# A two-block transformer kernel on one core: bias rows laid out in another stage, row stores waited for in another stage, and four weight loads issued ahead of sixteen small ones

## What is computed

```
# block 1
mod = silu(c) @ w_ada + b_ada                      # six rows of 1024: shifts, scales, gates
u   = layer_norm(x) * (1 + sc_m) + sh_m
q, k, v, f_logit, xb, gb = split(u @ w_in)
attn = forgetting_attention(q, k, v, f_logit + b_f)
lru  = rg_lru_branch(xb, gb, conv_w, conv_b, w_rg, b_rg, w_ig, b_ig, lru_lambda)
x   = layer_norm(ALPHA * x + (1 + gt_m) * (concat(rms(attn), rms(lru)) @ w_out))
x   = block with a mixture of 16 experts (2 per token), with sh_f, sc_f, gt_f
# block 2
mod_2 = silu(c_2) @ w_mod_2 + b_mod_2              # the same for the second block
bias  = rpb_2[:, row_off, col_off]                 # a relative position bias, looked up per head
...  neighbourhood attention with that bias, grouped attention, 32 experts (4 per token)
```

## Time and profile before

| what | value |
|---|---|
| median of 3 runs | 3181.14 us (3176.08 to 3182.53) |
| profiled execution, its own time | 3176.49 us |
| its span, first to last instruction | 3174.7 us |
| PE busy | 2540.7 us, 80% |
| DVE busy | 2245.4 us, 71% |
| ACT busy | 1558.6 us, 49% |
| POOL busy | 328.6 us, 10% |
| mean granted TensorE clock | 0.897 of full speed |

### The profile page before, as it was taken

The page is one execution under the profiler, slowest core; times in us unless marked ns, Lnnn a source line. Parts: engine busy times, 40 slices in busy tenths (PEclk is TensorE's granted clock), DMA queues, the critical chain, the costliest instruction groups (busy, mean ns, idle before and its releaser), DMA issues. The chain is left out here.

```text
span 3174.7 us, 37782 instructions
## 1 busy us (share of the span) xinstructions
PE 2540.7 (80%) x12807; PEld 2076.3 (65%) x12807; DVE 2245.4 (71%) x2177; ACT 1558.6 (49%) x1451; POOL 328.6 (10%) x277
## 2 busy tenths in 40 slices
PE   2968564499992699577885399999999999999991
PEld 2851554477771499466764377777777777777771
DVE  5546654588786312387844589999999999999985
ACT  2213430277671323255621066677776777777660
POOL 1120200033320000000000001110111111111110
PEclk9979786699996799788987599999999999999995
DMA  5736011499992322100021299999999999999984
GB/s 199 267 122 223 11 60 55 171 359 377 357 374 106 106 80 90 41 1 27 32 102 53 66 323 370 370 366 365 360 366 363 371 370 366 364 366 361 363 342 152
DMA packets 254857, 731.70 MB, mean 230 GB/s; under 512 B 29772, under 2 KB 69931, under 8 KB 252527
## 3 DMA queue, kind: packets, MB, share of 16 engines
q1 hardware_dynamic: 228180, 645.62, 56.3%
q0 software_dynamic: 21984, 80.77, 6.7%
q10 hardware_dynamic: 4608, 4.20, 0.4%
HBM read 692.73 MB, written 39.39 MB: 231 GB/s over the span
## 5 line engine op out<-in xcount | busy, mean ns | idle before, releaser
L48 PE MATMUL psum_all<-sb_ring_r,sb_arena_r 128*128 128x512 f32 (+1 forms) x2912 | 1068.7, 367 | 0.0
L152 DVE TENSOR_TENSOR sb_ring_r<-sb_ring,sb_hi_ring 128x2048 fp32r<-128x2048 f32 x297 | 674.5, 2287 | 251.5 <-ACT sb_hi_ring L143 246.1
L47 PE MATMUL psum_all<-sb_hi_ring,sb_arena_r 128*128 128x512 f32 (+1 forms) x1880 | 663.8, 353 | 49.9 <-DVE sb_ring_r L152 46.6
L49 PE MATMUL psum_all<-sb_hi_ring,sb_arena_r 128*128 128x512 f32 (+1 forms) x1880 | 659.6, 351 | 0.0
L143 ACT ACTIVATE sb_hi_ring<-sb_ring 128x2048 fp32r<-128x2048 f32 x297 | 563.6, 1912 | 107.7 <-DMA sb_ring<-in_w_gu_dram 35.0
L48 PEld LDWEIGHTS psum_all<-sb_ring_r,sb_arena_r 128*128 128x128 f32 x2912 | 556.6, 191 | 91.2
L152 DVE TENSOR_TENSOR sb_ring_r<-sb_ring,sb_arena_r 128x2048 fp32r<-128x2048 f32 x258 | 581.9, 2283 | 29.6 <-ACT sb_arena_r L143 29.1
L143 ACT ACTIVATE sb_arena_r<-sb_ring 128x2048 fp32r<-128x2048 f32 x258 | 484.9, 1910 | 199.7 <-DMA sb_ring<-in_w_gu_dram 194.8
L47 PEld LDWEIGHTS psum_all<-sb_hi_ring,sb_arena_r 128*128 128x128 f32 x1880 | 360.1, 192 | 106.5 <-DVE sb_ring_r L152 47.3
L47 PE MATMUL psum_all<-sb_arena_r 128*128 128x512 f32 x1032 | 417.7, 405 | 12.2 <-DVE sb_ring_r L152 7.0
L49 PE MATMUL psum_all<-sb_arena_r 128*128 128x512 f32 x1032 | 408.4, 396 | 0.0
(11 more groups left out here) (369 smaller groups left out, 3200.7 us busy)
## 6 DMA issues: line engine op xcount, KB each, us to landing
sb_ring<-in_w_gu_dram SPq DMA_DIRECT2D x272, 1024.0 KB, 6.8
sb_ring<-in_w_dn_dram SPq DMA_DIRECT2D x136, 1024.0 KB, 8.9
sb_ring<-in_w_e_gate_dram SPq DMA_DIRECT2D x36, 1024.0 KB, 7.5
sb_ring<-in_w_e_up_dram SPq DMA_DIRECT2D x36, 1024.0 KB, 7.3
sb_ring<-in_w_e_down_dram SPq DMA_DIRECT2D x36, 1024.0 KB, 7.8
sb_ring<-in_w_in_dram SPq DMA_DIRECT2D x27, 1024.0 KB, 5.8
sb_arena<-in_w_ada_dram POOLq DMA_DIRECT2D x16, 1024.0 KB
sb_ring<-in_w_mod_dram SPq DMA_DIRECT2D x16, 1024.0 KB, 5.1
```

Of the source, the lines that this page charges most:

```text
L47: eng.matmul(out, a[0], b[0], start=start, stop=False)
L48: eng.matmul(out, a[0], b[1], start=False, stop=False)
L49: return eng.matmul(out, a[1], b[0], start=False, stop=stop)
L152: dve.tensor_tensor(s.lo[c % SLOTS], s.raw[c % SLOTS], s.hi[c % len(s.hi)].bitcast(F32), ALU.subtract).then_inc(s.lo_made, 1)
```

## The change

Three edits. The first hunk is of `Modulation`, the second of `gates_and_lru` on SP, the third of `sync` in `forgetting_attention`, on SP too.

```diff
 class Modulation:
-    def store(self, pool):
+    def store(self, k, pool):
         for i, job in enumerate(self.jobs):
             if job[7] is not None:
                 pool.wait_ge(self.s.put, i + 1)
+                k.mod_stores += 1
                 pool.dma_start(job[7].rearrange("o (k p) -> p (o k)", p=P), job[5],
-                               allow_slow_non_contiguous=True).then_inc(self.s.stored, 16)
-        if self.rows:
-            pool.wait_ge(self.s.stored, 16 * self.rows)
+                               allow_slow_non_contiguous=True).then_inc(k.mod_stored, 16)
...
+            for n in range(MOD_SLOTS):
+                load_mod(n)
             for w, t in (("w_rg", w_r), ("w_ig", w_i)):
                 for half in range(2):
                     at_rows = slice(half * HW, (half + 1) * HW)
                     for j in range(NJ):
                         sp.dma_start(t[at_rows, j, at_rows], a[w][0, 2 * j + half]).then_inc(s.loaded, 16)
-            for n in range(len(mod_chunks)):
+            for n in range(MOD_SLOTS, len(mod_chunks)):
                 load_mod(n)
-            rows = k.rpb_rows.rearrange("(r i) (h g c) -> h r i g c", i=16, h=NH, c=48)
-            for h in range(NH):
-                for turned_row in range(GRID_H):
-                    first = RPB_PAD + (h * RPB_R + turned_row) * RPB_C - 16
-                    src = bass.AP(k.rpb_pad.tensor, first, [[1, 16], [RPB_C, GRID_H], [1, 48]])
-                    sp.dma_start(rows[h, turned_row], src).then_inc(k.rpb_rows_made, 16)
...
             for i, row in enumerate((2, 6)):
                 sp.dma_start(k.gate_rows[row:row + 1, :], mod_rows[32:33, i * D:(i + 1) * D]).then_inc(s.rows_stored, 16)
+            rows = k.rpb_rows.rearrange("(r i) (h g c) -> h r i g c", i=16, h=NH, c=48)
+            for h in range(NH):
+                for turned_row in range(GRID_H):
+                    first = RPB_PAD + (h * RPB_R + turned_row) * RPB_C - 16
+                    src = bass.AP(k.rpb_pad.tensor, first, [[1, 16], [RPB_C, GRID_H], [1, 48]])
+                    sp.dma_start(rows[h, turned_row], src).then_inc(k.rpb_rows_made, 16)
             sp.wait_ge(s.rows_stored, 48)
+            sp.wait_ge(k.mod_stored, 16 * k.mod_stores)
```

More of the change, by code:

```diff
@@ L294, in __init__ @@
         self.jobs, self.acc, self.psum, self.slots = jobs, acc, psum, slots
-        self.s = sems(nc, ctx, name, "used", "acc", "summed", "put", "stored", "chain")
+        self.s = sems(nc, ctx, name, "used", "acc", "summed", "put", "chain")
         self.landed = [nc.alloc_semaphore(name=f"{name}_landed{i}") for i in range(len(slots))]
@@ L304, in __init__ @@
         self.per = -(-len(self.steps) // turns)
-        self.rows = sum(job[7] is not None for job in jobs)
     def ready(self, u):
@@ L406, in _ @@
         def _(pool):
-            m.store(pool)
+            m.store(k, pool)
 def normalise(nc, k, name, src, ntt, width, dst, centre, eps, gain=None, bias=None, store=None, gate=None):
@@ L575, in _ @@
                 mod.load(pool)
-                mod.store(pool)
+                mod.store(k, pool)
         @block.sync
@@ L2652, in program @@
         k.rpb_rows = nc.dram_tensor("rpb_rows", (P, NH * GRID_H * 48), F32).ap()
+        k.mod_stored, k.mod_stores = nc.alloc_semaphore(name="mod_stored"), 0
         k.rpb_rows_made = nc.alloc_semaphore(name="rpb_rows_made")
```

## The result

| | before | after |
|---|---|---|
| median | 3178.61 us (4 runs, 3173.87 to 3182.53) | 3145.51 us (4 runs, 3140.77 to 3148.98) |
| ratio | | 0.9895, 95% interval 0.988 to 0.991 |
| span of the profiled execution | 3174.7 us | 3147.2 us |
| mean granted clock | 0.897 | 0.899 |

The change saves 33 us of the median; the spans of the two profiled executions differ by 27.5.

What follows compares the result with a forecast made beforehand. PE is busy 80%, mostly in untouched experts; the edits act on barrier-closed stages between 200 and 412 us, by who ends last. 24.4 + 7.8 + 2.6 = 34.8 us saved, giving 3141.7 to 3146.3, forecast 3145, range 3131 to 3151.

Steps and rivals of the forecast that it cites:

- Edit A: SP's 64 bias row DMAs move from the gate stage's end to the attention: ACT then ends the stage, 24.4 us saved.
- The cover in the attention: Attention work on PE, ACT and DVE hides SP's 64 issues: 55.6 us available, 41.1 needed.
- rival 4: SP issues the 64 DMAs more slowly and ends the attention; gain shrinks from 0.87 us each, slower from 1.41; chance 0.02.
- Edit C: In the gate stage, four chunk loads go ahead of the gate weights: 7.8 us saved on PE's chain.
- The pause: PE's wait for the first weight chunk in the gate stage, after the forget gate: 4.67 us to be saved.
- four take 13.2: PE's first four chunks in the gate stage take 13.2 us at full clock instead of 16.35, saving 3.1 us.
- Edit B: POOL no longer waits for the row stores at the projection's end; its DRAIN waits instead, 2.6 us saved.
- it ends at 222.9 + 0.08: POOL's DRAIN at the projection's end overlaps its walk with the last store's landing, ending at 223.0 instead of 225.6.
- Rival 1: POOL's DRAIN doesn't wait for the stores and the gate stage starts at once: gain 47.8 us, chance 0.13.
- Rival 2: DRAIN doesn't wait, but next stage's loads do; DVE gets b_f 6.4 us late: gain 41.4 us, chance 0.08.
- Rival 3: Chunks late or clock falls anyway, 4.7 or less instead of 7.8, b_f 2 us late: total gain 29.7, chance 0.13.

Runs made afterwards that it cites:

- A and C alone: Bias rows moved to the attention and four chunks loaded ahead of the gate weights, POOL still waiting for its row stores, against the kernel before: 3147.17 us, 0.9895.
- the kernel with the split loads: The kernel before, with each of POOL's 24 projection loads issued as two halves, so 54 DMAs instead of 30: 3182.62 us.

## Why the prediction was right, point by point

**Edit A, 24.4 us: right.** Timed alone it gave 24.3 (20.0 to 28.3), and the mechanism is seen in both traces: SP no longer ends the gate stage, ACT does, and the next stage follows 0.87 us later. The cover in the attention held: 0.66 us an issue, where rival 4 began to cost at 0.87.

**Edit C, 7.8 us: the right mechanism, a little too large.** The trace gives 6.5: the gate stage became 30.88 us shorter, of which 24.4 are put down to A. Timed alone it is 4.8 (1.6 to 8.0), which holds both numbers. The pause went, all 4.67 us. The other term, "four take 13.2", was mis-sized: I took the rate of twelve later chunks, and the first four take 13.9 us in every kernel that has edit C. That is 0.7 of the 1.3 us. The matmuls of both groups start 0.43 us apart; the twelve chunks look shorter in the rows because four of their 96 matmuls are recorded within 5 ns of another one, and why is not known. The lower clock thus cost the four chunks 16.35 - 13.90 = 2.45 us and not 3.1. The rest of the 1.3 is the forget gate, which I had left out of the sum as unchanged. PE was done with it 13.96 us into the stage, and now at 243.0, 14.65 us in. It begins 6.73 us into the stage in every run in which b_f is in time, at the lower clock level (0.63 us a matmul, 1.2 GHz). Its first matmul at the upper one (0.40 us, 2.4 GHz) comes 9.8 us into the stage in some executions and up to 12.3 in others: with edit C at 9.8, 10.1, 10.1, 11.5, 12.2, 12.3 and 12.3, without it at 10.1, 10.1, 11.0 and 11.1. With A and C alone the gate was done at 13.9 us, as before. So this 0.7 us lies within the scatter of the clock between executions, and no effect of the edit on it is shown.

**Edit B, 2.6 us: right that it is small and why, half the size.** The disputed step was that POOL's DRAIN waits for a transfer in flight, taken from 83 ns per DMA. The DRAINs of 21.3, 18.4 and 22.7 us in three executions, each ending 1.3 us behind the last landing, show that it waits, and so does the one of 20.9 us that stood for a load; the kernel with the split loads shows that the rate is per DMA. What failed is "it ends at 222.9 + 0.08": it ends 1.3 us behind, so 1.4 of the 2.6 us are left. This 1.4 is read from traces at equal landing; the times show no gain of B at all. Rival 1 needed a short DRAIN and falls.

**Rival 2** had a false premise here, the short DRAIN, but its mechanism is real, and it came true as soon as SP issued the stores: b_f 13.92 and 15.71 us late, more than the 6.4 I had priced, since there the last store went out just ahead of it. **Rival 4** stayed away in the changed kernel, and came with the stores in the attention, where 0.85 us an issue behind 14.4 us of stores let SP end the stage, 1 us behind a late ACT. **Rival 3** had C 5.1 us short, and it was 1.3 short.

**The sum.** 24.4 + 6.5 + 1.4 = 32.3 us, against 33.1 between the medians and a forecast of 34.8. The agreement is in part luck. In the profiled executions the landing was 3.4 us later after the change than before, which is most of why their spans differ by 27.5 only, and the medians hold landings of their own that no row shows. And the three edits timed one by one add up by their medians to 24.3 + 4.3 - 1.0 = 27.6 us, with intervals of several us each. So A is confirmed in size, C to within a few us, and B's 1.4 us by the trace alone.

## What to carry to other kernels

A wait that is taken away gains only if the barrier behind it doesn't wait for the same thing: read which instruction ends the stage on that engine, and what it counts. When a slow transfer is moved, ask what is issued behind it on any queue until it has landed, and put it where that is nothing or has slack; here the same six stores cost 19 us at a seam, some 13 us of an attention, and 3 us behind the last load of a stage. Issue work that nobody waits for belongs in the stage whose other engines end later than the queue, and its slack is read off before it is spent.

## What the runs showed of the hardware

- POOL's DRAIN at a stage's end takes 83 ns for each DMA that POOL issued in it (30, 37, 54 and 69 of them: 2.505, 3.082, 4.468 and 5.697 us), and with one in flight it ends 1.3 us after the landing.
- Six stores of 4 KB each, written 4 bytes at a time to DRAM, land 28 to 35 us after the first issue. With 64 bias rows issued beside them it takes longer: POOL's DRAIN behind them ended 52.6 us after the first issue (360.5 - 307.9). The DMA engines are idle for the last part of that: with the stores in the gate stage the windows (columns as above; the DMA share adds up transfer times and can pass 1) show them busy until 294, at 1 to 5 GB/s, while the load behind them came at 304.5.

```profile
282.00:288.00 6.00, 1.08 (x3) 0.09 (x1) 0.00 (x0) 3.96 (x3) 0.00 (x0) 1.00 1.99 1
288.00:294.00 6.00, 3.96 (x15) 3.66 (x15) 2.68 (x4) 3.60 (x6) 0.00 (x0) 0.50 1.30 5
294.00:300.00 6.00, 3.18 (x10) 2.47 (x11) 4.65 (x12) 3.15 (x8) 0.00 (x0) 0.50 0.09 1
```

- Issued by SP in a row, such stores take 0.5 to 1.0 us each in the median of three kernels, and the slowest of the six took 9.5, 9.8 and 11.5 us: the queue itself is held.
- While they pend beside the bias rows, engines that use no DMA for data stall for up to 18 us (PE, 337.7 to 355.9, with the stores issued by POOL in the attention). This was not expected, and its cause stays open.
